# A two-block diffusion and MoE network on one core: the recurrence's ACT and PE orders changed, part of the experts' transposes moved to VectorE, a loop hint dropped

## The reference, cut to what matters

```python
log_f = logaddexp(log(lb[d]), log1p(-lb[d]) + log_sigmoid(f))
k = -expm1(log_f)
S_t = diag(f_t) S_{t-1} + k_t v_t^T ;  o_t = S_t^T q_t      # both directions
```

```python
for e in range(8):
    out = out + gates[..., e:e+1] * ((silu(x @ w_gate[e]) * (x @ w_up[e])) @ w_down[e])
```

## Time and profile before

| what | value |
|---|---|
| median of 3 runs | 3162.36 us (3159.61 to 3163.47) |
| profiled execution: its own time | 3159.68 us |
| its span | 3157.9 us |
| mean granted TensorE clock | 0.987 |
| PE busy | 3022.1 us, 96% of the span |
| DVE, ACT, POOL busy | 732.6, 418.8, 246.2 us |
| mean DMA rate | 194 GB/s over the span |

### The profile page before, as it was taken

The page is one execution under the profiler, slowest core; times in us unless marked ns, Lnnn a source line. Parts: engine busy times, 40 slices in busy tenths (PEclk is TensorE's granted clock), DMA queues, the critical chain, the costliest instruction groups (busy, mean ns, idle before and its releaser), DMA issues.

```text
span 3157.9 us, 41336 instructions
## 1 busy us (share of the span) xinstructions
PE 3022.1 (96%) x18016; PEld 1707.5 (54%) x18016; DVE 732.6 (23%) x1705; ACT 418.8 (13%) x1026; POOL 246.2 (8%) x322
## 2 busy tenths in 40 slices
PE   6998899999999999899999999989999999999998
PEld 2445654444457777577656777454444444444434
DVE  1227822000046566410042000243000000000002
ACT  1105220000022212200031000131000000000001
POOL 1112300000012112100000000000000000000030
PEclk9999999999999999999999999999999999999999
DMA  8761012122121222153343334327999999999993
GB/s 341 285 250 39 1 67 80 40 100 80 40 79 52 67 54 61 63 192 123 137 174 120 140 140 159 128 84 287 359 403 379 380 403 380 381 403 380 381 404 132
DMA packets 211812, 613.32 MB, mean 194 GB/s; under 512 B 6252, under 2 KB 53580, under 8 KB 205104
## 3 DMA queue, kind: packets, MB, share of 16 engines
q1 hardware_dynamic: 204912, 592.20, 49.4%
q0 software_dynamic: 6256, 17.87, 1.7%
q10 hardware_dynamic: 464, 0.60, 0.1%
HBM read 603.43 MB, written 7.21 MB: 193 GB/s over the span
## 4 chain that ended last, share of the span: by engine, by line
PE 87%; DVE 5%; DMA 3%; issue 2%; ACT 2%; PEld 0%; PEldq 0%; POOLq 0%; POOL 0%; SPq 0%; DVEq 0%; ACTq 0%
PE ps_main L696 14%; PE ps_main L733 7%; PE ps_moe_down L3246 6%; PE ps_second L696 6%; PE ps_moe_gate L3196 6%; PE ps_moe_up L3196 6%; PE ps_main L2037 5%; PE ps_lin L1489 4%; PE ps_moe_down L3253 3%; PE ps_moe_up L3201 3%; PE ps_moe_gate L3201 3%; PE ps_second L733 3%; PE ps_main L583 2%; DVE rec_qd L2297 2%; PE ps_main L2060 1%
## 5 line engine op out<-in xcount | busy, mean ns | idle before, releaser
L696 PE MATMUL ps_main<-hT,ring_buf 128*128 128x256 f32 (+2 forms) x1408 | 448.0, 479 | 2.4 <-issue 1.6
L696 PEld LDWEIGHTS ps_main<-hT,ring_buf 128*128 128x128 f32 x1408 | 263.7, 190 | 188.3 <-issue 170.5
L2037 PE MATMUL ps_main<-ring_buf,hT 128*128 128x256 f32 (+2 forms) x992 | 227.2, 382 | 8.0 <-ACT hg_kT L2173 6.4
L733 PE MATMUL ps_main<-ring_buf,ffn_hiddenT 128*128 128x512 f32 x528 | 228.9, 593 | 2.0 <-issue 2.0
L696 PE MATMUL ps_second<-hT,ring_buf 128*128 128x256 f32 (+1 forms) x896 | 195.2, 380 | 4.0 <-DMA ring_buf<-in_w_ffn_up_dram 2.8
L2037 PEld LDWEIGHTS ps_main<-ring_buf,hT 128*128 128x128 f32 x992 | 166.2, 190 | 53.9 <-ACT hg_kT L2173 7.9
L696 PEld LDWEIGHTS ps_second<-hT,ring_buf 128*128 128x128 f32 x896 | 169.2, 192 | 31.0 <-issue 5.2
L3417 DVE TENSOR_TENSOR moe_hidden_buf<-moe_silu_buf,ps_moe_up 128x768 f32<-128x768 f32 (+1 forms) x32 | 27.3, 854 | 680.2 <-PE ps_moe_up L3201 680.2
L733 PEld LDWEIGHTS ps_main<-ring_buf,ffn_hiddenT 128*128 128x128 f32 x528 | 99.5, 190 | 127.8 <-issue 127.8
L1489 PE MATMUL ps_lin<-ring_buf,hT 128*128 128x448 f32 (+1 forms) x384 | 133.3, 500 | 0.0
L3196 PE MATMUL ps_moe_up<-ring_buf,moe_xg_buf 128*64 128x512 f32 (+1 forms) x672 | 131.8, 545 | 0.0
(11 more groups left out here) (550 smaller groups left out, 3553.3 us busy)
## 6 DMA issues: line engine op xcount, KB each, us to landing
ring_buf<-in_w_exp_down_dram SPq DMA_DIRECT2D x17, 4096.0 KB, 18.3
ring_buf<-in_w_exp_up_dram SPq DMA_DIRECT2D x16, 4096.0 KB, 18.5
ring_buf<-in_w_exp_gate_dram SPq DMA_DIRECT2D x15, 4096.0 KB, 19.8
mod_pieces<-in_mod_w_dram SPq DMA_DIRECT2D x40, 1024.0 KB, 6.4
moe_third<-in_w_exp_gate_dram SPq DMA_DIRECT2D x9, 4096.0 KB, 19.6
moe_third<-in_w_exp_up_dram SPq DMA_DIRECT2D x8, 4096.0 KB, 19.7
moe_third<-in_w_exp_down_dram SPq DMA_DIRECT2D x7, 4096.0 KB, 18.3
ring_buf<-in_odd_w_in_dram SPq DMA_DIRECT2D x40, 512.0 KB, 5.2
```

Source lines behind the costliest of these rows:

```text
L696: mm = nc.tensor.matmul(ps[:, lo:wide], view[:, k, i * P:(i + 1) * P], hT[:, k, first_col + lo:first_col + wide], start=k == 0, stop=k == ...
L733: mm = nc.tensor.matmul(ps_y[i % 2][:, h, :], hidT[:, b, i * P:(i + 1) * P], view[:, b, h * 512:(h + 1) * 512], start=first, stop=end)
L2037: mm = nc.tensor.matmul(ps[:, 0:width], hT[:, k, t * P:(t + 1) * P], view[:, k, 0:width], start=k == 0, stop=k == KD - 1)
```

## The change

It has four parts. (1) In the odd mixer ACT takes `kT` and `fT` before the table load and the logarithm and not after them. (2) There, PE does `f` 2 of the next head before `scores(u + 1)` and not after it. (3) In the experts, each narrow column tile j reads its weights as strips: 32 columns of every 128, beginning at 32j, and not a quarter of the columns at a stretch. The narrow half of `hid` then holds, in each block of 32 partitions, what a transpose of 32x32 blocks puts where `down` wants it. DVE does this with a new instruction after each `hidden`, into `narrowT` (two buffers); PE transposes only the wide half (4 and 2 tiles), and ACT copies only that. The narrow half of `down` waits for the new signal `moe_narrow`, and so does the next `hidden`. (4) The loop over further passes is built without the hint for the prefetch of its back edge, on all engines.

```diff
                     ahead(("f", 1))
                     scores(u)
+                    ahead(("f", 2))
                     scores(u + 1)
-                    ahead(("f", 2))
                     output(u)
@@ ACT, the first head; the loop over the heads has the same edit with h + 1
                 for kind, t in [("lb", 0)] + PROJECTED:
                     take(0, kind, t)
+                for kind, t in TURNED[:2]:
+                    take(0, kind, t)
                 logarithms(0)
-                for kind, t in TURNED:
+                for kind, t in TURNED[2:]:
                     take(0, kind, t)
@@ experts
-            hidT = sb(cx, "moe_hiddenT", [P, 6, P])
-            last_hidT = sb(cx, "moe_last_hiddenT", [P, 3, P])
+            hidT = sb(cx, "moe_hiddenT", [P, 4, P])
+            last_hidT = sb(cx, "moe_last_hiddenT", [P, 2, P])
+            narrowT = sb(cx, "moe_narrowT", [P, 2, 256])
@@ other_passes
-                with nc.Fori(FIXED, n_passes, engines=[eng.engine], hint_back_edge=True) as p:
+                with nc.Fori(FIXED, n_passes, engines=[eng.engine]) as p:
@@ PE, across
+                    in_strips = w.rearrange("p k (b j n) -> p k j b n", j=4, n=NARROW)
                             mm = nc.tensor.matmul(ps[j * 32:(j + 1) * 32, half:half + quarter], xg[:, k, WIDE:ROOM],
-                                                  w[:, k, j * quarter:(j + 1) * quarter], start=k == 0,
+                                                  in_strips[:, k, j, :, :], start=k == 0,
@@ PE, turned
-                    for i in range(PIECES[c][1] * 3 // 4 // P):
+                    for i in range(PIECES[c][1] // 2 // P):
@@ PE, down
+                    pe.wait_ge(S["moe_narrow"].handle, S["moe_narrow"].at(c + 1) + n0)
                     for b in range(blocks):
-                        x = mine[:, per2 + b % per4, b // per4 * 32:b // per4 * 32 + 32]
+                        x = narrowT[:, c % 2, b * NARROW:(b + 1) * NARROW]
@@ ACT, take_turned
-                    n = PIECES[c][1] * 3 // 4 // P
+                    n = PIECES[c][1] // 2 // P
@@ DVE, hidden
+                    dve.wait_ge(S["moe_narrow"].handle, S["moe_narrow"].at(c) + n0)
                     n = PIECES[c][1] * 3 // 4
                     nc.vector.tensor_tensor(hid[:, 0:n], silu[:, 0:n], ps_u[:, 0:n], ALU.mult)\
                         .then_inc(S["moe_hidden"].handle, 1)
+                    dve.wait_ge(S["moe_hidden"].handle, S["moe_hidden"].at(c + 1) + n0)
+                    half = PIECES[c][1] // 2
+                    nc.vector.transpose(narrowT[:, c % 2, 0:n - half], hid[:, half:n])\
+                        .then_inc(S["moe_narrow"].handle, 1)
```

More of the change, by code:

```diff
@@ L2221, in _ @@
                             take(h + 1, kind, t)
+                        for kind, t in TURNED[:2]:
+                            take(h + 1, kind, t)
                         logarithms(h + 1)
-                        for kind, t in TURNED:
+                        for kind, t in TURNED[2:]:
                             take(h + 1, kind, t)
@@ L2825, in program @@
         ("moe_gate", "tensor"), ("moe_silu", "scalar"), ("moe_up", "tensor"), ("moe_hidden", "vector"),
+        ("moe_narrow", "vector"),
         ("moe_turned", "tensor"), ("moe_hidden_T", "scalar"), ("moe_down", "tensor"), ("moe_ye_a", "scalar"),
@@ L3240, in down @@
                     blocks, w = width // P, room_of(DOWN_ITEM[c], p, width // P, D)
-                    per2, per4 = blocks // 2, blocks // 4
+                    per2 = blocks // 2
                     mine = hidT_of(c)
```

## The result

The changed kernel takes 3134.55 us (median of 4 runs, 3128.68 to 3134.56), beside 3162.91 for the kernel before on the same chip (4 runs). The medians lie 28.4 us apart. The ratio is estimated as 0.9916, 95% interval 0.9903 to 0.9928, which is 26.6 us, between 22.8 and 30.7. The forecast of 3138.5 was a ratio of 0.9923, or 24 us. Its case came true, and the range holds the time. The profiled execution has a span of 3132.7 us, 25.2 less than before.

The account below looks back on a forecast made before the run. The prediction took PE, with 87% of the chain, as the bound. Savings of 7.9 + 9.3 - 0.7 + 5.9 = 22.4 us from 3159.68 gave 3137.3, or 3140.0 against the runs' median; it put 3138.5 between, range 3132 to 3148.

Parts of the forecast that it names:

- Its case: Whole kernel: the outcome as forecast, faster at 3138.5 us, none of the rivals happening; chance 0.71.
- Part 1, 7.9 us: Odd mixer: ACT's earlier copies remove PE's 0.99 us wait before `i` 1 in all 8 heads, without a new wait.
- Part 2, 9.3 - 0.7 us: Odd mixer: `f` 2 ahead of `scores(u+1)` saves 1.33 us in 7 heads, less 0.1 a head for a new wait.
- The new wait: Odd mixer: PE waits before `output(u+1)` for DVE's `merge` and `take`, 0.1 us a head, bounds 0 and 0.3.
- the 0.4 us: Odd mixer: DVE's query products gain this from 1 us less overlap with POOL's keys, at 0.45 rather than 0.80 each.
- Part 3, 5.9 us: Experts: seven fewer PE transposes save 0.77 us in each of 7 written-out passes, plus 0.55 in the looped pass.
- The 0.55 of the looped pass: Experts, looped pass: saving left after 0.22 us merely lengthens the wait before the second `up`.
- The strided reads, nothing: Experts' narrow matmuls: reading weights in strips costs nothing; the rival that they are slow had chance 0.07.
- the DVE transposes, hidden: Experts: DVE's transposes after `hidden` delay nobody, cost nothing; 32 x 0.63 = 20 us if not covered.
- the two reasons for the first: Strided reads: gaps come only once in 32 elements, and four column tiles abreast already read slowly; cost nothing.
- Part 4, nothing: Loop's back edge: dropping the hint changes nothing, within 1 us, as PE waits 2.13 us at the exit anyway.

Follow-up runs that it names:

- f2_first: The kernel before with only PE's `f` 2 moved ahead of `scores(u + 1)`, ACT's order unchanged: 3148.28 us, ratio 0.9963.
- experts_only: The kernel before with only the experts' strips, DVE transposes and fewer PE transposes: 3156.64 us, ratio 0.9983.
- no_hint_only: The kernel before with only the loop's back-edge prefetch hint left out: 3160.35 us, ratio 1.0003.
- copies_first: The kernel before with only ACT's `kT` and `fT` copies moved ahead of the table load and logarithm: 3146.10 us, ratio 0.9953.
- half_narrow: The changed kernel without half of the narrow products of `gate` and `up` (4 of 8 k), so PE has less work: 3101.29 us.

## Why the prediction was right

**Part 1, 7.9 us.** The wait went in all 8 heads, as the step said, and nothing became late: no idle of L2037 is put down to `hg_kT`. The term was somewhat low. From `i` 0 to `qT` it gave 8.7 us in the 8 heads (41.47 to 32.79), just within its upper bound of 8.8. Alone, the part also gave 0.46 a head through DVE, which the prediction saw as help for part 2 only. In the whole change that 0.46 is not to be had again, since part 2 removes the rest of the same wait.

**Part 2, 9.3 - 0.7 us.** The step from 8.37 to 7.04 was met with 7.03. Over the 7 heads it gave 10.1 us (59.26 to 49.19) and not 9.3: the term took one head to stand for all, and that was the head with the shortest wait, 1.08 us where the six others had 1.17 to 1.21. The new wait was taken as 0.1 a head, between 0 and 0.3: f2_first shows 0.35 without part 1, and the changed kernel 0.06 with it, 0.45 us in all for the 0.7. DVE is free at 1105.57, which is 7.04 after `scores(u)`; about 7.1 was forecast. The argument that the wait depends on POOL's overlap with DVE fits these runs: with the keys started sooner DVE is in time, and without that it is late. POOL's keys began 1.65 us sooner, counted from ACT's first freedom, where about 2 was said. What the rows do not bear out is that the 0.4 us comes from DVE's block products: L2301's x4 in direction 0 took 3.09 us against 3.19. Most of the relief came in the instruction behind them, 0.48 and not 0.91.

**Sum of the odd mixer.** Heads: 8.7 + 10.1 - 0.4 = 18.3. The stage shows 17.7, since what lies behind the last head's `qT` took 62.25 us and not 61.61, at a granted clock of 0.92 and not 0.94. Over the eight executions that have both edits it is 17.1 to 18.7. Forecast 16.5.

**Part 3, 5.9 us.** Seven written-out passes gave 0.77 each, 5.4 in all, as forecast; experts_only has 5.0 in its stage. The 0.55 of the looped pass did not come in this pair. The step there counted only one wait. It left out that the clock may fall behind it, which cost 1.37 us, and the wait of 0.70 before a `down`, which went. That the first wait would grow (2.77; 2.9 was said) is within the scatter of the runs. The stage shows 3.7 and not 5.4 because of a place outside the change: the first `gate` of the first pass took 8.78 us and not 7.09, again at a lower clock.

**The strided reads, nothing,** and **the DVE transposes, hidden**: both as said, the first shown by 206.98 us. Of the two reasons for the first only that of the long runs held.

**Part 4, nothing:** 1.0003. The wait behind the loop is still 2.13 us (2.18 in no_hint_only).

**The rest.** The steps sum to 22.4 us, and their measured values to 18.3 + 5.4 = 23.7. The ratio says 26.6 and the span fell by 25.2. Of this 3.8 came in a stretch that the change does not touch, and the edited stages gave 21.4. That the ratio lies as near the forecast as it does is in part luck. Two stretches that no edit reaches show why its interval is 8 us wide. From the kernel's first product of L1489 to L260 the thirteen profiles of this case took between 343.8 and 349.4 us. The layers between the two stages took between 820.1 and 829.4, and there the time goes with the granted clock. Their windows, in the kernel before and in f2_first (columns as in the earlier trace rows):

```profile
1349.00:2177.19 828.19, 794.07 (x3191) 528.39 (x3190) 157.98 (x553) 107.08 (x321) 21.19 (x42) 0.98 0.38 141
```

```profile
1343.56:2163.70 820.14, 784.21 (x3191) 522.88 (x3190) 157.64 (x553) 106.63 (x321) 21.11 (x42) 1.00 0.38 142
```

So the parts' own ratios (14.9, 11.7, 5.4 and -0.9 us, together 31) can't be added up to better than this; the stretches of the heads and of the passes can.

## What to carry to other kernels

When an engine's copy is all that another waits for, put it ahead of the long table load and logarithm that nobody needs yet, and look at what then runs beside the engines behind: here POOL out of DVE's way was worth 0.46 us a head in one order and 0.29 in the other. Two small edits can depend on each other, so cost the new wait of the one with and without the other. Where a stage repeats, read the same wait in all its repeats before one stands for all. Where the weights' loads have only a microsecond of margin, look for small indirect transfers in the same stretch, and move these before you shorten the arithmetic.

## What was not expected of the hardware

**A moving operand with single float32 values 16 bytes apart** doubled the matmuls, from 206.98 to 421.06 us, even with four column tiles abreast; the median of a single matmul rose from 379 to 632 ns. With two wanted values in every 16 bytes it was 216.68 to 219.54.

**The clock behind a wait for weights is not settled by the wait's length.** In the looped pass the `up` behind it took 7.09 us after waits of 2.03, 2.50, 2.64 and 2.82 us, but 8.78 after 2.54, 8.46 after 2.77, 8.71 after 2.92, and 8.78 after 3.04 and 3.60. The longest wait without a fall is that of copies_first:

```profile
3011.57 7.09 PE L3200 MATMUL ps_moe_up<-moe_third,moe_xg_buf 128*64 128x512 f32 x32 [2.82 <-DMA moe_third<-in_w_exp_up_dram]
```

In half_narrow, 2.63 was followed by 8.78 and 2.77 by 7.09. What decides, these runs do not show. Whether it falls is worth up to 1.7 us, twice what a pass gains by part 3.
